# Expert-search queries as three passes over split operands, with most weight rests made on GpSimd

## The reference, cut to what matters

```
def block(xb):                                    # a block of tokens
    q = (xb @ w_query).reshape(t, PEER_HEADS, 2, PEER_HALF)      # 8 heads, 2 x 128 columns each
    scores = jnp.einsum('thpd,hpnd->thpn', q, sk)                # 2 x 128 keys
    s_val, s_idx = lax.top_k(scores, PEER_TOPK)                  # 16 of 128, then 16 of 256 pairs
    ...
    act = jax.nn.gelu(jnp.einsum('thkd,td->thk', expert_u[expert], xb))
    return jnp.einsum('thk,thkd->td', gate * act, expert_v[expert])
```

## Time and profile before

| | |
|---|---|
| three runs, median (lowest to highest) | 2827.73 us (2824.94 to 2829.92) |
| the profiled execution, its own time | 2825.03 us |
| its span in the trace | 2823.2 us |
| TensorE busy | 2795.2 us, 99% |
| VectorE busy | 2334.7 us, 83% |
| ScalarE busy | 1045.3 us, 37% |
| GpSimd busy | 747.1 us, 26% |
| mean granted TensorE clock | 0.998 |

### The profile page before, as it was taken

How to read it: one execution, slowest core, us unless ns; L and a number is a source line. 1 busy time by engine, 2 the same in 40 slices (tenths; PEclk the granted TensorE clock), 3 DMA queues, 4 the chain that set the end, 5 groups by cost and what they waited for, 6 DMA issues and landing times.

```text
span 2823.2 us, 40525 instructions
## 1 busy us (share of the span) xinstructions
PE 2795.2 (99%) x15010; PEld 1572.8 (56%) x15010; DVE 2334.7 (83%) x4390; ACT 1045.3 (37%) x1382; POOL 747.1 (26%) x518
## 2 busy tenths in 40 slices
PE   9999999999999999999989999999999999999999
PEld 5455555556666444444467775555566664444444
DVE  6954899997888899999733568999978888999996
ACT  2253222234555333333342442323345553333333
POOL 0000233321111454544100002333301115545450
PEclk9999999999999999999999999999999999999999
DMA  4213678767998999999512246878679979999993
GB/s 159 89 47 144 240 274 294 277 245 274 312 309 283 391 394 399 392 399 396 207 64 90 77 155 242 315 255 310 246 268 316 312 294 396 395 400 392 397 397 147
DMA packets 214838, 776.05 MB, mean 275 GB/s; under 512 B 15508, under 2 KB 101912, under 8 KB 194744
## 3 DMA queue, kind: packets, MB, share of 16 engines
q1 hardware_dynamic: 50096, 416.89, 38.7%
q0 software_dynamic: 73728, 268.47, 25.8%
q10 hardware_dynamic: 90888, 89.14, 9.2%
HBM read 681.90 MB, written 92.54 MB: 274 GB/s over the span
## 4 chain that ended last, share of the span: by engine, by line
PE 92%; DVE 2%; ACT 2%; issue 1%; DMA 1%; PEld 1%; DVEq 0%; PEldq 0%; POOL 0%; ACTq 0%; SPq 0%
PE ps L1966 31%; PE ps L1896 12%; PE ps L1897 12%; PE ps L1895 12%; PE ps L1869 8%; PE ps L1483 3%; PE ps L1571 2%; PE ps L1948 2%; PE ps L1947 2%; PE ps L1520 1%; PE ps L1521 1%; PE ps L1524 1%; PE ps L1905 1%; PEld ps L1966 1%; PE ps L1667 1%
## 5 line engine op out<-in xcount | busy, mean ns | idle before, releaser
L1966 PE MATMUL ps<-arena 128*128 128x512 bf16 x4584 | 990.7, 379 | 3.8 <-ACT arena L760 2.5
L521 POOL DMA_INDIRECT arena<-in_ur,arena x256 | 348.8, 1362 | 1556.0 <-DVE arena L1188 934.2
L1966 PEld LDWEIGHTS ps<-arena 128*128 128x128 bf16 x4584 | 448.1, 98 | 545.2 <-issue 3.0
L1161 DVE TENSOR_TENSOR arena<-arena 128x1024 bf16<-128x1024 f32 x512 | 611.5, 1220 | 116.9 <-ACT arena L760 94.2
L1897 PE MATMUL ps<-xnh,arena 128*128 128x384 bf16 x2048 | 667.6, 326 | 0.0
L1896 PE MATMUL ps<-xnl,arena 128*128 128x384 bf16 x2048 | 667.5, 326 | 0.0
L1895 PE MATMUL ps<-xnh,arena 128*128 128x384 bf16 x2048 | 667.4, 326 | 0.0
L760 ACT ACTIVATE arena<-arena 128x1024 bf16<-128x1024 f32 x512 | 524.2, 1048 | 120.7 <-PE ps L1966 97.3
L521 POOL DMA_INDIRECT arena<-in_v,arena x256 | 397.4, 1552 | 402.6 <-DVE x_res L1197 342.2
L1197 DVE SCALAR_TENSOR_TENSOR x_res<-arena,x_res 128x1024 f32<-128x1024 f32 x256 | 328.6, 1283 | 21.1 <-issue 0.9
L786 ACT ACTIVATE arena<-ps 128x384 f32<-128x384 f32 x256 | 125.6, 491 | 563.8 <-PE ps L1897 563.7
(11 more groups left out here) (247 smaller groups left out, 2534.1 us busy)
## 6 DMA issues: line engine op xcount, KB each, us to landing
arena<-in_v SPq DMA_DIRECT2D x64, 2048.0 KB, 10.4
arena<-in_u SPq DMA_DIRECT2D x62, 2048.0 KB, 10.4
h_scratch<-arena ACTq DMA_DIRECT2D x60, 768.0 KB
arena<-h_scratch SPq DMA_DIRECT2D x60, 768.0 KB, 8.6
arena<-gate_scratch SPq DMA_DIRECT2D x64, 640.0 KB, 6.9
arena<-in_wmix SPq DMA_DIRECT2D x14, 2048.0 KB, 7.8
gate_scratch<-xnT ACTq DMA_DIRECT2D x10, 2048.0 KB
gate_scratch<-arena ACTq DMA_DIRECT2D x10, 2048.0 KB
```

The costliest lines, as they stand in the source:

```text
L521: pool.indirect_dma_start(ring[n % NBUF], None, ur_d[L] if g < P else vr_d[L], at).then_inc(gat_in[n % NBUF], 16)
L1161: dve.tensor_tensor(lo[:, s], raw[s // TPG][:, s % TPG], hi[:, s], ALU.subtract).then_inc(lo_ready, 1)
L1966: last = pe.matmul(ps[:, 2 + 2 * tt + dh], c, v[:, TPG * s + q, dh * 512:(dh + 1) * 512], start=start and c is ch and v is hi, stop=stop a ...
```

## The change

All query products of both PEER stages use split operands in float32r and three passes instead of float32 products:

- ScalarE rounds each head's query weights (`query_high`, two copies of 128x1024), behind the GELU of tile 8h+5 for the next head, at the start of the stage for head 0.
- The rests of the weights, `wq_lo = wq - wq_hi`, two subtractions of 128x1024, are made by VectorE for head 0 and by GpSimd for heads 1 to 7. GpSimd's list has them for head h+1 ahead of gather 12h. They are written over `wq`.
- VectorE makes the rests of x (`query_rest`): for block 0 from PSUM in eight pieces, for blocks 1 to 3 with a copy and a subtraction over 128x1024. `x_rest` takes the memory of `x`, so ScalarE's queue first writes each block of x to DRAM (`x_keep`), and SP reads all four back after the last head's queries (`q_done`), ahead of the loads of u groups 16 and up.
- The dots stand where they were in VectorE's list.

```diff
+        x_rest = rounded("x_rest", ARENA + KD * T + KD * TD, TT, KD, P)
+        wq_lo = rounded("wq_lo", A_X, KD, 2 * P)
+        wq_hi = [rounded("wq_hi0", A_X + 2304, KD, 2 * P)] + [rounded("wq_hi1", A_GR, KD, 2 * P)] * (PH - 1)
@@ block.sync, peer_loads
                     head_load(h + 1)
                     stream_load(u_d[L, h * 2 + 3], h * 2 + 3, 1)
+                sp.wait_ge(q_done, PH * (L + 1))
+                for tt in range(TT):
+                    sp.dma_start(x[:, tt], x_keep[tt]).then_inc(x_back, 16)
                 with sp.Fori(PH - 1, 2 * PH - 1) as h:
@@ block.gpsimd
-            for g in range(2 * P):
-                gather(0, g)
+            def query_low(L, h):
+                for p in range(2):
+                    at = slice(4 * p, 4 * p + 4)
+                    pool.wait_ge(q_high, 2 * (PH * L + h) + p + 1)
+                    pool.tensor_tensor(wq_lo[:, at], wq[:, at], wq_hi[h][:, at].bitcast(F32), ALU.subtract).then_inc(q_low, 1)
+
+            def gathers(L):
+                for g in range(2 * P):
+                    if g % 12 == 0 and g // 12 + 1 < PH:
+                        query_low(L, g // 12 + 1)
+                    gather(L, g)
@@ block.scalar
+                if k % 2:
+                    act.dma_start(x_keep[tt], x[:, tt]).then_inc(x_kept[tt], 16)
...
+            def query_high(L, h):
+                act.wait_ge(wq_in, 16 * (PH * L + h + 1))
+                for p in range(2):
+                    at = slice(4 * p, 4 * p + 4)
+                    act.activation(wq_hi[h][:, at], wq[:, at], ACT.Copy).then_inc(q_high, 1)
...
+                    if n % RING == 5 and n < NK // 2 - RING:
+                        query_high(L, n // RING + 1)
@@ block.vector
+            def query_rest(k, tt):
+                at = slice(tt * P, (tt + 1) * P)
+                dve.wait_ge(xt_low, TT * k + tt + 1)
+                dve.drain()
+                if tt:
+                    src = xs[:, tt].rearrange("p (k t) -> p k t", t=P)
+                    dve.tensor_copy(x_hi[:, :, at], src)
+                    dve.wait_ge(x_kept[tt], 16 * (k // 2 + 1))
+                    dve.drain()
+                    dve.tensor_tensor(x_rest[:, tt], src, x_hi[:, :, at].bitcast(F32), ALU.subtract).then_inc(xt_rest, 1)
+                    return
...
+                    if step == 2:
+                        query_low(m, 0)
@@ block.tensor, peer
-                def queries(s, at):
-                    for kd in range(KD):
-                        last = pe.matmul(ps[:, 2 + s, at], wq[:, kd, s * P:(s + 1) * P], xnT[:, kd, at],
-                                         start=kd == 0, stop=kd == KD - 1)
-                    return last
+                def queries(h, s, tiles):
+                    at = slice(tiles.start * P, tiles.stop * P)
+                    cols_at = slice(s * P, (s + 1) * P)
+                    bank = ps[:, 2 + s, at]
+                    pe.wait_ge(q_high, 2 * (PH * L + h + 1))
+                    for kd in range(KD):
+                        pe.matmul(bank, wq_hi[h][:, kd, cols_at], x_hi[:, kd, at], start=kd == 0, stop=False)
+                        pe.matmul(bank.rearrange("p (a t) -> p a t", t=P), wq_hi[h][:, kd, cols_at], x_rest[:, tiles, kd],
+                                  start=False, stop=False)
+                    pe.wait_ge(q_low, 2 * (PH * L + h + 1))
+                    for kd in range(KD):
+                        last = pe.matmul(bank, wq_lo[:, kd, cols_at], x_hi[:, kd, at], start=False, stop=kd == KD - 1)
+                    return last
```

More of the change, by code:

```diff
@@ L289, in build @@
         xt_rest = sem("xt_rest")
+        q_high = sem("q_high")
+        q_low = sem("q_low")
+        x_kept = [sem(f"x_kept{tt}") for tt in range(TT)]
+        x_back = sem("x_back")
         w_high = sem("w_high")
@@ L527, in _ @@
             pool.memset(g_z, 0.0).then_inc(pool_prep, 1)
-            for g in range(2 * P):
-                gather(1, g)
+            gathers(1)
         @block.scalar
@@ L887, in norm_high @@
                     at = (kd - KD // 2) * P
[L888 to L889 removed]
+                    dst = xnT if k == 0 else x_hi
+                    dst = xs[:, tt, kd * P:(kd + 1) * P] if k % 2 and tt else dst[:, kd, tt * P:(tt + 1) * P]
+                    last = dve.tensor_scalar(dst, ps[:, turn_bank(k, tt) + 1, at:at + P],
                                              cols[:, C_GAIN + KD * k + kd:C_GAIN + KD * k + kd + 1], None, ALU.mult)
@@ L1451, in turned @@
                     pe.wait_ge(xt_high, 2)
+                if k % 2 and tt == 2:
+                    pe.wait_ge(xt_rest, TT * (k - 1) + 1)
                 if k % 2 and tt >= 2:
@@ L1914, in peer @@
                     tile(h * RING, 0)
-                    pe.wait_ge(wq_in, h * 16 + 16 * (PH * L + 1))
                     for s in range(2):
-                        last = queries(s, slice(0, T))
+                        last = queries(h, s, slice(0, TT))
                     last.then_inc(q_done, 1)
```

47 lines of the change are left out of this document (29 added, 18 removed).

## The result

| | before | changed |
|---|---|---|
| median (lowest to highest) | 2828.13 us (2824.94 to 2829.92) | 2884.92 us (2878.08 to 2889.52) |
| ratio, 95% interval | | 1.0201 [1.0188, 1.0213] |
| the profiled execution, its own time | 2825.03 us | 2881.74 us |
| mean granted TensorE clock | 0.998 | 0.982 |

The change costs 57 us, 2.0%. The forecast said slower, with 10 us lost; the time lies outside its range.

A forecast was written before the change was run, and what follows sets the result against it. VectorE's list (45.88 us a head) was taken as the bound close behind TensorE's 46.72. Layer 0 at -3.4 and layer 1 at -6.4 us lose 9.8: 2834.8 us for a profiled execution, 2837.5 as median; range 2808 to 2860.

The forecast's parts named there:

- The two bounds: In a head, TensorE is busy 46.72 us and VectorE's list takes 45.88, so a shorter TensorE meets VectorE after 0.84 us.
- What TensorE saves: Head queries in three passes: 2.84 us less per head, period 43.88 us; 2.4 less in head 0; 44.6 us over both layers.
- GpSimd's price and c: One GpSimd subtraction priced at 2.2 us; c, VectorE's time lost to both in a head, taken as 2.2 (bounds 0, 4.4).
- The sum for a layer: TensorE's lead over its old times at head 7: a + 13.6 - 5c - d, taken as a + 1.6 us.
- 5 x (0.84 - c): Heads 1 to 5: five VectorE lists, each changing TensorE's lead by 0.84 us less the hold c, taken as 2.2.
- 2.84 behind the wait in head 7: Head 7's queries: TensorE gains its full saving of 2.84 us behind its wait for the rests.
- The run-ahead: Heads: TensorE may run ahead of VectorE by 3.7 us, less a delay d of the rests of 1 us.
- A transfer of that size landed in 4.8 us: Stage start, layer 0: ScalarE's write of x's block 3, begun at 249.4, would land at 254.2 us.
- both stage starts: From stage start to the end of head 0's queries: layer 0 gains 0.5 us, layer 1 loses 2.5.
- The late group of u: End of head part: group 16 lands at 610.2, TensorE waits 6.4 us for tile 58's GELU (bounds 1.2, 11.6); 5.5 taken.
- a heavier hold alone: Rival: GpSimd's hold full or its subtraction longer than priced (c over 3.3); at c = 4.4, 2859.5 us; chance 0.09.
- rival 1: In the heads GpSimd gives way, not VectorE (c under 0.7): 2813.5 us at c = 0, faster; chance 0.25.

The follow-up runs named there:

- experiment 11: The changed kernel without the third pass (products of the weights' rests); GpSimd still makes the rests and TensorE waits for them ahead of the scores: 2844.87 us, ratio 1.0060.
- experiment 3: The changed kernel with the weights' rests of heads 1 to 7 made by VectorE too, none by GpSimd: 2887.72 us, ratio 1.0214.
- Experiment 12: The kernel of experiment 9, with SyncE waiting for the write of x's last block behind the first 0.5 MB tile of u: 2824.59 us, ratio 0.9992.
- Experiment 1: The changed kernel with x read back only behind the loads of all u groups: 2866.21 us, ratio 1.0127.
- experiment 9: The changed kernel with ten dots a head, x read back behind u's loads, and head 1's rests ahead of the first gather: 2825.88 us, ratio 0.9992.
- experiment 8: The changed kernel with x read back behind u's loads, x's write ahead of them, and nine dots a head instead of twelve: 2876.46 us, ratio 1.0169.
- experiment 10: The kernel of experiment 9 with the rests two gathers earlier and ScalarE's high parts of the query weights one tile earlier: 2852.99 us, ratio 1.0085.
- experiment 4: The kernel before, plus two GpSimd subtractions of 128x1024 in the same 14 places, one input read twice, result unused: 2832.62 us, ratio 1.0016.

## Why the prediction was right in sign and wrong in size

**The two bounds: right.** The single wait of 0.84 us in the earlier trace rows told that VectorE is the next bound, and 11 shows it alone: 48.1 us a head when TensorE needs 40.3.

**What TensorE saves: right.** Its own period is 43.91 us (forecast 43.88).

**GpSimd's price and c: nearly right.** One subtraction takes 2.36 us (priced 2.2 from rows far off; the estimate by the GPSIMD Engine Reference of the Trainium skill, 1.96 times VectorE's 1.22 us, was 2.4, and the trace agrees). The hold is 2.63 us a head where c was taken as 2.2, by the very order described: the second subtraction gets in before the two-input instruction and holds it for its whole length (c = 2.8 there). Over ten heads that is 4 us.

**The sum for a layer: wrong in VectorE's five lists and in what stands behind the wait in head 7.** Forecast -1.6 us a layer for heads 1 to 7, measured by TensorE's own ends +8.3 and +8.0. The step that failed is the term 5 x (0.84 - c): from the end of head 2's rests to the end of head 7's pass 249.0 and 248.5 us, 49.8 and 49.7 a head, where 45.88 + 2.2 = 48.1 was forecast. That is 8.5 and 8.1 us a layer. The larger hold makes 2 of it. The rest are VectorE's waits for gathered rows, 5.7 and 5.4 us in these stretches, which the forecast put at nothing; in experiment 11 the same five lists have no such wait and take 242.7 and 242.6 us. They stand mostly at the sixth of the six dots at the turn of a head: the gather that starts at 370.77, when the first of these dots has freed a buffer, lands at 381.0, beside a load of u of 2 MB, and VectorE waits 3.69 us for it. The kernel before has no such wait from head 2 on. It is not GpSimd's subtractions that make the gathers late, for they also come late in experiment 3, which has none. What sets the moment at which they meet the loads of u stays open. The other term that failed is "2.84 behind the wait in head 7": 2.3 and 2.5 us of it went at the lower clock. The run-ahead was 3.9 us (359.68 less 355.82), more than the 2.7 taken.

**"A transfer of that size landed in 4.8 us": wrong.** The reads at the program's start that I took it from ran beside one another and beside weights (the DMA engines' share is over 0.9 from 2 us on), six of the eight writes had the engines to themselves and landed in 2.6 us, and the last write of a layer shares them with 4 MB of u and landed in up to 9.4 us. I looked at the size of the transfer and not at what was in flight with it. Forecast for both stage starts +2.0 us, measured +12.3 by the copies and +15.5 by TensorE's own ends, of which the two waits are 10.6 us and the lower clock behind them 3.7 us (24 products of 256 columns in 4.72 and 4.64 us, at 0.119 each 2.86). The 3.0 us that the forecast gave to the copy and subtraction ahead of layer 1's normalised blocks came: TensorE waits 3.7 us for these blocks at the end of mixer 1, where it waited 0.6. Experiment 12 shows that the cost is not the write's place but the room: with the write in time, the loads are late.

**The late group of u: right mechanism, clock left out.** The wait of 6.5 us a layer is the 6.4 us that the sum gave before I took 5.5. But it cost 9.5 us and more, since TensorE came back at the lower clock. Experiment 1 returns 18.7 us for both.

**The lower clock: missing from the forecast.** No step priced it. All waits of TensorE were counted at their length. Behind nine of the ten waits for the weights' rests, 2.78 to 4.33 us long, the way to the copy took 1.7 to 2.7 us more than head 2's 7.45; behind the tenth, of 3.41 us, it took 0.1 us more. With the two levels, a mean of 0.982 means that TensorE was at 1.2 GHz for 0.036 of the span, 104 us, against 0.004 (11 us) before. Part of these 104 us lies in the waits themselves; at half speed the rest accounts for the 39 us by which its busy time fell less than by the 44.6.

**The start of the program: 7.3 us, not the change's.** In eight kernels with the same instructions up to that point the first query product starts between 247.0 and 254.2 us (the kernel before: 246.9), and the changed kernel's profile has the latest; its clock was 0.80 and 0.94 in the first two stretches of 20 us, where the kernel before has 1.00. A typical run of the changed kernel has less of this item; its median (2884.92 us) is nonetheless above the profiled execution's 2881.74, and the ledger can't say where the typical run has the difference.

The chances put 0.51 on slower, and that came, but not by the forecast balance: the heads were to gain 1.6 us a layer, and they lost 8, so the sign was right by the two ends alone. The range stopped at 2860 us since its upper end was worked out from a heavier hold alone: it had the unknown price of one mechanism in it and not the price of being late, which all the mechanisms share. Its lower end is also added wrongly: rival 1's 2813.5 us with 1.2 instead of 5.5 us in each layer gives 2804.9, not 2808, which changes nothing here.

## What to carry to other kernels

When a change moves an engine from the bound to just behind another engine, shorten the list of the one that it now meets in the same edit: here two dots a head moved to a stage with room, and the reads of x behind the loads, turned 57 us lost into no loss. Choose the place of GpSimd's subtractions by what VectorE runs when they start: the same two cost it 2.6, 4.7 or 5.2 us a head. Price a new wait of TensorE of 3 us at more than its length, with the work behind it at half speed. Read a transfer's duration from a row in which the same other transfers are in flight, and ask of each load that is moved what stands in the same queue behind it.

## What the runs showed of the hardware

- Behind a wait of TensorE of 3.53 us, as behind one of 5.40 us, the work ran at the lower level (half speed) for 4 to 5 us. One wait of 3.41 us had no such stretch behind it. In the heads the periods of both layers are 55.6 us above TensorE's own in sum, of which 35.0 us are waits; in experiment 9 it is 18.4 us with 11.2 of waits. These waits thus cost about 1.6 times their length.
- A write of 0.5 MB on ScalarE's queue landed in 2.6 us alone and in 9.4 us beside four loads of 0.5 MB and one of 2 MB on SyncE's queue; with the loads behind the first 0.5 MB held back it took 3.0 us at most. DMA: Bandwidth & Descriptors of the Trainium skill (Queues, rings and completion order) says that an engine takes turns between queues that have work; the trace shows that the smaller transfer can still take 3.6 times as long.
- Two subtractions of GpSimd, 4.7 us in sum, hold the instruction of VectorE that starts beside them. A split with two inputs lost 2.6 us when it started inside the first of them and 4.7 us when it started 0.1 us ahead of it (experiment 8). A cast with one input was held for 5.2 us (experiment 10), while the searches and maxima with one input kept their times beside the subtractions.
- On GpSimd the same subtraction took 2.36 us with a rounded float32 result and two different inputs, and 1.97 us with one input read twice (experiment 4).
